# First norm and modulation rows taken in step with their transfers, modulation rows spread through two double norms, and weight lowering moved to VectorE in the second attention

## What is computed

```
mod = silu(c) @ w_ada[l] + b_ada[l]            # shift, scale, gate; the same for c_ctx
h   = layernorm(x) * (1 + sc1) + sh1
x   = layernorm(ALPHA * x + g1 * mixer(h), ln1_g, ln1_b)
h   = layernorm(x) * (1 + sc2) + sh2
x   = layernorm(ALPHA * x + g2 * ffn(h), ln2_g, ln2_b)
```

```
win   = kv[idx] + pos_emb                      # 15 windows of 32 tokens, step 16
k_cmp = gelu(win @ w1) @ w2                    # the same for v_cmp
o     = gate0 * o_compressed + gate1 * o_selected + gate2 * o_window
```

## Time and profile before

| | |
|---|---|
| time, median of 3 runs | 2849.3 us (2849.01 to 2853.16) |
| the profiled execution | 2850.67 us, span 2848.9 us |
| TensorE busy (PE) | 2730.2 us, 96% |
| VectorE (DVE), ScalarE (ACT), GpSimd (POOL) busy | 1330.3, 1285.9, 1368.9 us |
| chain that ended last | TensorE 81%, VectorE 11%, ScalarE 4%, DMA 1%, GpSimd 1% |
| read from HBM | 357.59 MB, 126 GB/s over the span |

### The profile page before, as it was taken

One profiled execution on the slowest core, in us unless ns is written; L12 is line 12 of the kernel. 1 busy time (PEld: TensorE's weight loads), 2 busy tenths in 40 slices (PEclk: granted clock), 3 DMA queues, 4 the chain that ended last, 5 costly groups with the idle time before them and its releaser, 6 DMA issues.

```text
span 2848.9 us, 42737 instructions
## 1 busy us (share of the span) xinstructions
PE 2730.2 (96%) x17758; PEld 2325.7 (82%) x17758; DVE 1330.3 (47%) x2602; ACT 1285.9 (45%) x2181; POOL 1368.9 (48%) x616
## 2 busy tenths in 40 slices
PE   7999999999999999999999999999999999998999
PEld 5777877688887787887878879989987699885997
DVE  2778867541333211103767664453126464156541
ACT  3254443423523422224464445644454566554664
POOL 3332021244442444442831428758864278752787
PEclk9999999999999999999999999999999899999999
DMA  6332022133233434334520225535553345543464
GB/s 243 109 122 100 31 68 80 53 114 108 89 126 113 166 131 150 121 96 146 176 86 16 82 66 178 168 109 181 182 193 111 111 156 185 164 145 111 149 185 155
DMA packets 104074, 361.42 MB, mean 127 GB/s; under 512 B 11143, under 2 KB 18567, under 8 KB 103369
## 3 DMA queue, kind: packets, MB, share of 16 engines
q1 hardware_dynamic: 103880, 358.68, 38.4%
HBM read 357.59 MB, written 1.05 MB: 126 GB/s over the span
## 4 chain that ended last, share of the span: by engine, by line
PE 81%; DVE 11%; ACT 4%; DMA 1%; POOL 1%; issue 1%; SPq 0%; DVEq 0%; ACTq 0%
PE PS L381 81%; DVE AR L2092 1%; DVE PS L2100 1%; ACT AR L1369 1%; DMA RING<-w_ada_in 1%; DVE AR L2097 1%; DVE AR L2288 1%; POOL RINGL L2943 1%; PE PS L392 1%; DVE AR L2096 1%; DVE SM L2362 1%; DVE XT L2092 1%; ACT WH L1349 1%; DVE AR L2751 1%; ACT AR L1921 0%
## 5 line engine op out<-in xcount | busy, mean ns | idle before, releaser
L2943 POOL TENSOR_TENSOR RINGL<-RING,WH 128x1024 fp32r<-128x1024 f32 x548 | 1303.7, 2393 | 1411.7 <-ACT WH L1349 1391.0
L1349 ACT ACTIVATE WH<-RING 128x1024 fp32r<-128x1024 f32 x548 | 569.1, 1045 | 686.2 <-PE PS L381 565.5
L381 PE MATMUL PS<-HTR,WH 128*128 128x256 f32 (+2 forms) x2736 | 807.6, 320 | 0.0
L381 PE MATMUL PS<-HTH,WH 128*128 128x256 f32 (+1 forms) x2336 | 683.2, 319 | 4.1 <-POOL HTR L2948 2.5
L381 PEld LDWEIGHTS PS<-HTR,WH 128*128 128x128 f32 (+1 forms) x2736 | 519.8, 190 | 39.7 <-issue 1.8
L381 PEld LDWEIGHTS PS<-HTH,WH 128*128 128x128 f32 x2336 | 445.3, 191 | 44.0 <-issue 14.1
L381 PE MATMUL PS<-ARR,WH 128*128 128x512 f32 (+1 forms) x1856 | 441.0, 340 | 3.5 <-ACT WH L1349 2.6
L381 PE MATMUL PS<-HTH,RINGL 128*128 128x256 f32 (+1 forms) x2336 | 402.6, 315 | 2.3 <-POOL RINGL L2943 2.2
L381 PEld LDWEIGHTS PS<-HTH,RINGL 128*128 128x128 f32 x2336 | 342.2, 191 | 31.2 <-POOL RINGL L2943 3.7
L381 PEld LDWEIGHTS PS<-ARR,WH 128*128 128x128 f32 x1856 | 310.9, 189 | 46.2 <-issue 5.6
L1369 ACT ACTIVATE AR<-PS 128x512 f32<-128x512 f32 (+6 forms) x344 | 163.6, 494 | 297.6 <-PE PS L381 287.9
(11 more groups left out here) (227 smaller groups left out, 3326.8 us busy)
## 6 DMA issues: line engine op xcount, KB each, us to landing
RING<-w_ada_in SPq DMA_DIRECT2D x96, 512.0 KB, 3.6
RING<-w_up_in SPq DMA_DIRECT2D x88, 512.0 KB, 3.6
RING<-w_gates_in SPq DMA_DIRECT2D x48, 512.0 KB, 3.4
RING<-w_ff_gate_in SPq DMA_DIRECT2D x44, 512.0 KB, 4.2
RING<-w_ff_up_in SPq DMA_DIRECT2D x44, 512.0 KB, 4.3
RING<-w_down_in SPq DMA_DIRECT2D x44, 512.0 KB, 3.6
RING<-w_glu_in SPq DMA_DIRECT2D x32, 512.0 KB, 5.6
RING<-w_ff_down_in SPq DMA_DIRECT2D x32, 512.0 KB, 3.5
```

The source lines that it names most:

```text
L381: return e.matmul(out_, lhsT, rhs, start=start, stop=stop)
L1349: e.activation(RINGS[name][:, j, 0:width], RING[:, b % NSLOT, 0:width], ACT.Copy).then_inc(*a_upper.up(b))
L2943: e.tensor_tensor(RINGL[:, i, 0:width], RING[:, i, 0:width], RINGS[name][:, j, 0:width], ALU.subtract).then_inc(*g_lower.up(b))
```

## The change

Six edits.

1. The input is one tensor of `x` beside `ctx`, loaded in two transfers of four feature tiles each, and the first norm's sums wait for each half. TensorE starts with 20 `hum` matmuls.
2. `first_norm` replaces the first `layernorm` and `fill_all`: the sixteen blocks of modulation rows are taken one at a time between the steps of the norm, with two `hum` matmuls after each of the last nine. The 18 `hum` behind it become 12.
3. In `layernorms` the bias sum is made by a reduction on VectorE and one matmul behind the variance, in place of eight matmuls ahead of the means; the copy of `SHIFT` on ScalarE moves with it.
4. In layer 0 the calls of `fill` are spread: one behind the mean's spread, one behind the variance (where 5 `hum` were), one behind the next mean's spread, and in the first double norm one more in the middle of the second variance. The `hum` ahead of each of the eight tiles of the second variance are 1 where they were 3 (at some tiles none; in the second double norm of layer 0 all eight now have one).
5. VectorE lowers the first three blocks of the program, and in `attention2` the twelve blocks of `w_in2` and four of `w_mix` of each layer, each at the end of the round before its use. GpSimd leaves them out.
6. The windows are prepared one tensor at a time in rounds 9 and 10, half of the copies on ScalarE, and `compress_hidden` waits for its own tensor alone.

```diff
-            def project(name, l, ct, src, ready, cols, until, kt_total=8, order=range(8)):
+            def lowered(n, by):
+                if by is d_lower:
+                    dve_lowers.add(n)
+                pe.wait_ge(*by.to(n))
...
-                    pe.wait_ge(*g_lower.to(n))
+                    lowered(n, by)
...
-                o = take("means", *pid, until=(a_norm, "shift", *pid))
-                for k in range(8):
-                    mm(o[:, 256:257], M1024, col(f"ln{i}_b", l, k), k == 0, k == 7)
+                o = take("means", *pid, until=(a_norm, "mean", *pid))
...
-                fill(1)
-                hum(1 if l == 0 else 4)
+                if l == 0:
+                    fill(1)
+                else:
+                    hum(4)
...
-                hum(5)
+                o = take("shift", *pid, until=(a_norm, "shift", *pid))
+                pe.wait_ge(*d_norm.to("shift", *pid))
+                mm(o[:, 0:1], M1024, BIAS_SUM, True, True).then_inc(*p_norm.up("shift", *pid))
+                if l == 0:
+                    fill(1)
+                else:
+                    hum(5)
...
-                    fill(3 if i == 1 else 2)
+                    fill(1)
...
-                    if l or k >= 4:
-                        hum(3)
+                    if pid == ("p", 0, 1) and k == 4:
+                        fill(1)
+                    if l or i == 2 or k > 4:
+                        hum(1)
...
+            def first_norm():
+                nid = "m", 0, 1
+                rows = (b for a in range(4) for b in ada_blocks(a))
+                hum(20)
+                o = take("means", *nid, until=(a_norm, "mean", *nid))
+                for k in range(8):
+                    pe.wait_ge(*x_in[k // 4].to("half"))
+                    t = in_strips(o, XT[:, k, :], k == 0, k == 7)
+                t.then_inc(*p_norm.up("means", *nid))
+                next(rows)
...
+                for _ in rows:
+                    hum(2)
+                ada_turn(0)
...
+            def lower_block(b):
+                _, width, name, j, _ = blocks[b]
+                dve.wait_ge(*a_upper.to(b))
+                tt(RINGL[:, b % NSLOT, 0:width], RING[:, b % NSLOT, 0:width], RINGS[name][:, j, 0:width],
+                   ALU.subtract).then_inc(*d_lower.up(b))
...
+                    if i + 1 in TILE_AT:
+                        lower_rows("w_in2", TILE_AT[i + 1])
+                    if i + 1 in MIX_AT:
+                        lower_rows("w_mix", MIX_AT[i + 1])
...
-            e.dma_start(XT[:, :, 0:256], A["x"]).then_inc(*x_in.up("x"))
-            e.dma_start(XT[:, :, 256:512], A["ctx"]).then_inc(*x_in.up("all"))
+            for i in range(2):
+                e.dma_start(XT[:, 4 * i:4 * i + 4, :], A["x"][:, 4 * i:4 * i + 4, :]).then_inc(*x_in[i].up("half"))
```

More of the change, by code:

```diff
@@ L173, in signal @@
             return signals[-1]
-        const_in, x_in, x_again = (signal(n, 16) for n in ("const_in", "x_in", "x_again"))
+        const_in, x_again = (signal(n, 16) for n in ("const_in", "x_again"))
+        x_in = [signal(f"x_in{i}", 16) for i in range(2)]
         sums_in, masks_in, rope_in = (signal(n, 16) for n in ("sums_in", "masks_in", "rope_in"))
@@ L365, in tensor @@
             phases.clear()
+            dve_lowers.clear()
             def take(*label, until):
@@ L482, in ada_rows, with ada_blocks @@
             def ada_rows(a):
+                for _ in ada_blocks(a):
+                    pass
+            def ada_blocks(a):
                 u = a // 4
@@ L495, in ada_rows @@
                         t.then_inc(*p_block.up(n))
-                if a % 4 == 3:
-                    p_block.also("ada", u)
+                        if a % 4 == 3 and (k, half) == (7, 1):
+                            p_block.also("ada", u)
+                        yield
             def ada_turn(u):
@@ L611, in layernorms @@
                 hum(9 if mid == ("m", 0, 2) else 7)
+            def first_norm():
[8 more added lines that the diff above has]
+                next(rows)
+                o = take("mean", *nid, until=(d_norm, "sub", *nid, 3))
+                pe.wait_ge(*a_norm.to("mean", *nid))
+                out_of_strips(o, MEAN, 512).then_inc(*p_norm.up("mean", *nid))
+                next(rows)
+                next(rows)
+                o = take("var", *nid, until=(a_norm, "sd", *nid))
+                for h in range(4):
+                    pe.wait_ge(*a_norm.to("sq", *nid, h))
+                    for k in (2 * h, 2 * h + 1):
+                        t = in_strips(o, SQN[:, k, :], k == 0, k == 7)
+                    if h < 3:
+                        next(rows)
+                t.then_inc(*p_norm.up("var", *nid))
+                next(rows)
+                o = take("rstd", *nid, until=(d_norm, "mul", *nid, 7))
+                pe.wait_ge(*d_norm.to("rstd", *nid))
+                out_of_strips(o, RSTD, 512).then_inc(*p_norm.up("rstd", *nid))
+                for _ in rows:
+                    hum(2)
+                ada_turn(0)
             def gla_gates(l, seq, tile):
@@ L1126, in mix_block @@
                                n == 0 and side is src[0], False)
-                pe.wait_ge(*g_lower.to(b))
+                lowered(b, by)
                 for t in range(2):
@@ L1884, in tile2, with compress_windows @@
                     *a_mix.up("raw", l, i))
+            def compress_windows(l, a):
+                sig, what = qk_ready(WINDOW_TILES[a])
+                act.wait_ge(*sig.to(what, l, WINDOW_TILES[a]))
+                for g in range(2):
+                    t = copy(TK[0:64, a, g, :], QK[64 * g:64 * g + 64, WINDOW_TILES[a], :])
+                t.then_inc(*a_mix.up("tk", l, a))
             def compress_sums(l, a):
@@ L2592, in vector @@
             ada_at[:] = 0, 0, 4
-            dve.wait_ge(*x_in.to("all"))
+            for half in x_in:
+                dve.wait_ge(*half.to("half"))
             for l in range(DEPTH):
@@ L2602, in vector @@
                         affine(1, BOTH, k)
+                    for n in range(3):
+                        lower_block(stage_block["w_glu", 0, n % 2 * 8 + n // 2])
                     ada_at[:] = 4, 4, 12
```

91 lines of the change are left out of this document (49 added, 42 removed).

## The result

The changed kernel takes 2835.05 us (median of 4 runs, 2832.67 to 2839.39). The kernel before took 2851.07 beside it (4 runs, 2849.01 to 2853.16). The ratio is 0.9949, with a 95% interval of 0.9931 to 0.9967: faster by .5%. I had forecast 2819, in 2807 to 2831. The sign was right, the gain about half of what I had said.

The account below looks back on a forecast made before the run. TensorE, on the chain for 81% of the span, was taken as the bound. Gains 8 + 8 + 4.3 + 4.7 + 5 = 30.0 us off 2850.67 gave 2820.7, with the median 1.4 lower 2819; range 2807 to 2831.

Parts of the forecast that it names:

- The start: From the inputs to the first product: earlier sums and modulation blocks no longer in lumps gain 8 us, bounds 4.4 and 10.
- TensorE uses a block in 2.78 / 6 = .46 us: Start: TensorE's time for one modulation block, read from the earlier trace, .46 us.
- nine blocks are left, each .46 with two `hum`: Start, behind the first norm's last spread: a block with its `hum` costs 1.0 us, so the last is used at 33.3.
- the rival on the clock: Start and double norms: fewer `hum` drop TensorE to the lower clock, a block costs 1.7, total 2829 us; chance .12.
- Layer 0's double norms: Removing the `COL` matmuls from the front and spreading the blocks gains 8 us behind the mixer and 4.3 at the second place.
- the root can then follow the last squares within .5 us: Layer 0's first double norm: ScalarE's root no longer waits 8.58 us for TensorE, upper bound of gain 9.6 us.
- Layer 1's double norm: Wait of 3.64 us cut to .3, plus 1.4 from the front: gain 4.7 us.
- there the shorter `hum` gives it: Layer 1's double norm: fewer `hum` ahead of the tiles bring the gain of 4.7 us.
- The second attention: Both layers: removed waits and lower clock give 15.8 us, new waits for lowered blocks cost 11; net 5, bounds -1 and +10.
- The price of the odd rounds: Second attention: TensorE waits for VectorE's lowered blocks in five odd rounds, 1.1 us each, 5.5 a layer, 11 in all.
- behind scores that hide a lowering: Second attention, rounds of `w_mix`: lowerings on VectorE cost nothing; without that cover 8 x 1.16 us.
- the start's lower bound of 4.4: Start: inputs, small tensors and sixteen blocks, 11.2 MB at 324 GB/s, limit the gain to 4.4 us; as rival Bytes chance .05.

Follow-up runs that it names:

- experiment 2: Changed kernel with the first three blocks lowered by GpSimd again and the start's last nine modulation blocks in pairs with four `hum`: 2830.4 us (.9930).
- experiment 1: Changed kernel with the first three blocks of `w_glu` lowered by GpSimd again instead of VectorE: 2832.0 us (ratio .9939).
- experiment 5: Changed kernel with GpSimd lowering the sixteen blocks of each second attention again, windows still one tensor at a time: 2834.6 us (.9947).
- experiment 7: Changed kernel with VectorE lowering the block for an odd round ahead of the rotation instead of behind it: 2823.1 us (.9900).
- experiment 8: Changed kernel with 18 `hum` behind the first norm in place of 12, nothing else: 2835.0 us (.9948).
- experiment 9: Changed kernel with first three blocks on GpSimd, modulation blocks in pairs, and 18 `hum` behind the first norm: 2830.2 us (.9935).
- experiment 10: Changed kernel with GpSimd's first three blocks, paired modulation blocks, two `hum` a tile in layer 1's norm, early odd-round lowerings, 18 `hum`: 2817.8 us (.9878).
- experiment 3: Changed kernel with three `hum` ahead of each tile of layer 1's double norm in place of one: 2834.36 us (.9945).
- experiment 4: Changed kernel with two `hum` a tile in layer 1's double norm in place of one: 2834.52 us (.9946).

## Why the prediction was wrong, point by point

**The start: 8 forecast, .3 measured, and 3.5 lost behind it.** Two steps failed. The first is "TensorE uses a block in 2.78 / 6 = .46 us", carried to "nine blocks are left, each .46 with two `hum`". The .46 is a block's price when blocks stand together. One alone costs .98, and experiment 2 shows a pair for the same price. Nine blocks so took 9 x 1.62 = 14.6 us in place of 9; that is the 5.6 us. The row that should have stopped me is in the earlier trace rows: four matmuls, one block, at 38.99 took 1.92 us, and I put all of that down to the clock, which was half of it. The same trace has a block alone at the higher clock, which I had not looked at:

```profile
23.30 1.05 PE L381 MATMUL PS<-RING,SCP 128*32 128x512 f32 x4 [1.05 <-DMA RING<-w_ada_in]
```

In the rival on the clock I had a block at 1.7, and the 1.62 looks like it, but the cause isn't the clock: the granted clock from 24 to 40 us was 1.00. The second step is an edit that I never costed: the first three lowerings, on VectorE. They met GpSimd's `HTR` and held it 3.4 us (4.65 - 1.30); experiment 1 gets 2.4 of it back at the first product. I had quoted the rule that VectorE operations with two inputs in SBUF and GpSimd operations exclude each other for a whole instruction (the Trainium skill, "SBUF — State Buffer", SBUF: two separate sides), but asked only whether a lowering would wait, not whom it would make wait. The trace agrees with the exclusion here: `HTR` ends 1.1 us behind VectorE's third lowering (48.37 against 47.26), and alone it takes 1.30. That section also lets the one that starts first keep the other out; the row of `HTR` begins .05 us ahead of VectorE's (43.72 against 43.77), so that part these rows don't show.

**Lower clock behind the wait.** Behind 5.05 us of standing the first nine products were slow: 1.9 us. Another 1.6 were lost near 195 us, .4 of which came back, where TensorE was at the lower clock in nine of the eleven traces of the changed kernel and its variants, though it was busy as long as before (19.31 of 20 us). I had no term for either.

**Layer 0's double norms: 8 and 4.3, measured 6.4 and 3.5.** The mechanism was right and the size somewhat off. The step that failed is "the root can then follow the last squares within .5 us": in the first it stands 3.5 us behind them, in the second 1.05 (I had .3). In 930 to 934 the granted clock was .59, and the matmuls of the last four blocks took 3.66 us for what takes 1.9 elsewhere. But this is the smaller part. In the six traces in which the clock stayed at 1.00 through this norm (experiments 1, 5, 7, 8, 9 and 10) the same code still leaves the root 2.7 to 3.1 us behind. ScalarE's roots here and in experiment 5:

```profile
936.40 0.37 ACT L1445 ACTIVATE RS<-PS,COL 128x128 f32<-128x128 f32 x1 [3.54 <-PE PS L386]
```

```profile
936.80 0.37 ACT L1445 ACTIVATE RS<-PS,COL 128x128 f32<-128x128 f32 x1 [2.74 <-PE PS L386]
```

What I had left out is the order: the last four blocks stand ahead of the sums of tile 4, so when they end, about with the squares, TensorE still has four tiles of sums and three `hum`, 2.7 us of unbroken work in experiment 5 (934.02 to 936.7).

**Layer 1's double norm: 4.7, measured .6.** The failed step is "there the shorter `hum` gives it". The clock fell, and one `hum` at 1.2 GHz filled the time of three at 2.4. This was my rival on the clock, put at .12, whose condition names few `hum` in the double norms but whose price leaves layer 1's out. Experiments 3, 4 and 8 show it: three `hum` at the higher clock take 12.8 us, two 11.2, one 10.2 where the clock held and 12.6 to 13.8 where it fell. The front without `COL` gave its part, 1.5 us, and the slower tiles took .9 of it back.

**The second attention: 5, measured 10.1.** The price of the odd rounds was right: waits of 4.9 us a layer against 5.5, .54 in round 3 against .55, a lowering of 1.217 against 1.16. The sixth wait, 1.06 us a layer for a block of `w_mix`, I had put at nothing, "behind scores that hide a lowering"; so the 6.0 a layer come near 5.5 partly by luck. The gain was undersized: the term that was too small is what the two waits and the clock behind them cost. One source: from the window in the earlier trace rows I took 2.0 us for one stretch of lower clock in each layer, but layer 0 had another in 2240 to 2260, with a granted clock of .78 before and 1.00 after, that I had not looked at. Its mask products lie 10.1 us apart there before and 7.1 after: 3.0 us. About half of this is chance: in the seven traces of the changed attention this gap is 7.1 three times and 8.6 to 8.8 four times. Against my reading of the cause stands experiment 5: in the steady gaps the move to VectorE is worth .4 us of the 7.0, because its waits eat what it gives. The rest came with the copies on ScalarE and either the split or the move; what the copies do alone is not shown.

**The range** missed because the start's lower bound of 4.4 was a bound on transfers alone, and no bound at all on TensorE's own time for the blocks. It was also narrower than its own terms: the lower ends that the prediction names (4.4, 4.8, 1.5, 3.6 and -1) add up to a gain of 13, which is 2836, while the range stopped at 2831. The other end was off as well, as the three upper ends named give 2811 and not 2808.

## What to carry to other kernels

Ask of every duration that you divide by a count whether the instructions overlapped; take the price for the new arrangement from a row in which they stand as they will. When work moves to an engine that shares a resource, list what it will stand beside and make late, not only what it waits for. Filler work that keeps TensorE's clock up costs no time while the engine would wait anyway, so taking it out should be priced as the work behind it at half the clock. Filler ahead of an input is another matter: there it must end before the input lands, at either clock. And where a helper's result comes just too late, try its place in the queue before its engine: experiment 7 moved one call and gained 12 us.

## What the hardware showed that I had not expected

Matmuls of 32 columns by 512 that write different strips of a bank overlap so fully that two blocks cost what one costs (1.06 and 1.05 us). VectorE's lowerings held a GpSimd operation from 1.30 to 4.65 us, and GpSimd's lowering held a VectorE operation on 128x16 from .17 to 2.11. The granted clock is not the same from run to run at marginal places: the same double norm with the same matmuls took 12.6 to 13.8 us in seven traces and 10.2 in one, and the second double norm of layer 0 took 14.3 in ten and 20.1 in one. Such places can make up a good part of the 2 to 13 us by which four runs of one kernel differ; as one run of each has a trace, this is argued.
